# Gates between the heads' pairs, setup steps at other places, forgetting logits in float32r, and squares summed by TensorE

## The chip, the cores and the metric

The kernel runs on one core of one Trainium2 chip, as one launch. The metric is the device time in microseconds. Before the change it is 1714.79 us, the median of three runs (1713.35 to 1715.84).

## The reference

The input is one sequence of 256 tokens with 1024 features. Two blocks follow each other, each with two layers, in fp32.

```
first block, per layer:
  mod = c @ mod_w + mod_b                -> six vectors: shift, scale, gain, twice
  h = rmsnorm(x)*(1+scale) + shift ; p = h @ w_in
  sparse attention: 8 heads of 64 over the 64 keys of highest score; the score is a
    weighted sum of relu(q_i . k_i) over 8 indexer heads
  forgetting attention: 8 heads of 64, logits = q.k/8 + cum[q] - cum[k], causal,
    cum = running sum of log_sigmoid(f + bias)
  x += gain * (sigmoid(g_a)*y_a + sigmoid(g_b)*y_b) @ w_out
  x += gain * (silu(conv a) * conv b of rmsnorm(x) @ w_up) @ w_down
x = rmsnorm(x)
second block, per layer:
  h = rmsnorm(x) @ w_in_2, and from it five branches: gated linear recurrence (forward and
    backward), conformer convolution, short convolution, window attention, cross attention
    to a memory of 256 tokens
  x += rmsnorm((sum over branches of sigmoid(h @ w_gate) * (y @ w_branch)) @ w_out)
```

## The kernel before, in words

Activations lie with features on the partitions: `x` is 128 x 8 x 256. Every large product takes its operands as a high and a low part in float32r: `w_hi`, `w_lo` for weights and `h_hi`, `h_lo` (or `a_`, `y_`, `o_`, `m_`) for activations. `linear` (L1213 to L1219) issues three matmuls per 128 rows: high by high, low weight by high, high weight by low; one output tile of 128 columns of a 1024-row matrix is 24 matmuls of 128x256. `token_major` (L1251 to L1257) does the same with weights as the moving side. Small products are fp32 matmuls; the profile shows each of them as two records.

Weights come from HBM in chunks of 1 MB into a ring of five, all issued by SP in one order (L1171), each when the chunk five before it has been used. Two blocks of eight 128x128 tiles are in a chunk. ScalarE copies a block into `w_hi` (L1496), VectorE subtracts it into `w_lo` (L1819), six blocks ahead of their use; both do that in `split_to`, before the work of each step. Modulation weights are chunks of their own: a step `mod` multiplies a quarter (256 outputs) straight from the ring with 16 records (L1292), ScalarE copies the result to `modacc` (L1536), and `modred` sums it over partitions by matmuls with ones (L1302), 16 records for the eight columns of one vector; VectorE adds the bias.

One function, `plan()`, writes a single list of steps; each engine walks it and does its part of each step in that order. A step claims one of seven PSUM banks in turn, and waits until the bank's result of seven claims before has been taken (`wait_taken`).

- **Start.** `stats` squares x on ScalarE (L1524) and GpSimd adds five squares into `mean` (L1117); `root` sums that and the three other squares over partitions (L1275, L1278), and ScalarE (Ln L1530, Exp L1532) and VectorE (L1901 to L1907) make 1/sqrt. `norm` then makes `h_val` (VectorE L1926, the last of eight tiles by GpSimd), `h_hi` (ScalarE L1552) and `h_lo` (VectorE L1922), and the first four token-major products run as one group, for which the low halves of blocks 0 to 3 must stand. ACT_TABLE_LOAD stands in `root` (L1528).
- **Tables.** The step `setup` comes behind three pairs of token-major products. VectorE writes `rel_rep` (L1854), then angles; TensorE multiplies the buckets (L1265, fp32, 32 rows), VectorE adds into `line`, ScalarE takes the sines.
- **First block's attention.** After the pairs `qa` and the first value pair come `cum` (TensorE L1320 to L1322, for which VectorE writes `lf`, L1980) and `decay2` (VectorE, L1991: eight `lhs` tiles of 16 partitions); then the indexer (L1331), q and k tiles of the forgetting attention (`qkf`, ScalarE L1602 into `h_val`) with a `topk` on VectorE after each four. `att` issues the logits of four pairs of heads (L1344, for the forgetting attention followed by L1346, the 16-row bias product), VectorE masks and reads them out (L2048), ScalarE takes exp. 16 gate tiles (`gate1`, 24 matmuls each) are filled in: two between the two forgetting attentions, three in each `att_out`, one behind each of the last two `att_turn`. After each second gate one modulation quarter follows.
- **Second block.** The layer's input norm squares x as it is updated; VectorE (for the first layer) or GpSimd (for the second) adds the squares. The products `hf` of the recurrence follow the last `att_turn` (L1380, transposes of `o_tm`) and the gate `az`.

## Time and profile before

| what | value |
|---|---|
| median of three runs | 1714.79 us |
| profiled execution | 1720.28 us |
| its span, first to last instruction | 1718.5 us |
| TensorE busy | 1589.4 us, 92% |
| VectorE / ScalarE / GpSimd busy | 66% / 48% / 3% |
| mean granted clock of TensorE | 0.943 of 2.4 GHz |
| read from HBM | 284.75 MB, 167 GB/s |

Matmuls overlap in the pipeline, so the start-to-start distance of two rows tells the pace better than the duration of one. A granted clock of 1.00 is 2.4 GHz, 0.50 is 1.2 GHz; a value between is a mean over a stretch with both. Idle time in brackets at the end of a timeline row is that of the engine just before the row, with what ended it.

### The profile page before, as it was taken

How to read it: one execution, taken by the hardware profiler on the slowest of the kernel's cores; microseconds unless marked ns; L12 is line 12 of the kernel's file. 1: busy time of each engine (PE TensorE's matmuls, PEld its weight loads, DVE VectorE, ACT ScalarE, POOL GpSimd, SP SyncE). 2: the span in 40 equal slices, each digit the busy share in tenths (PEclk: the TensorE clock that was granted, in tenths of full speed). 3: DMA queues.
4: the chain of work that ended last, by engine and by line, in shares of the span. 5: the costliest groups of instructions: out<-in, count | busy, mean ns of one | idle time of the engine just before them, and what ended most of it. 6: DMA issues, size and time to landing. Idle time of an engine off the chain costs nothing. (4 is left out here: it accounts for less than half of the span.)

```text
span 1718.5 us, 31556 instructions
## 1 busy us (share of the span) xinstructions
PE 1589.4 (92%) x12784; PEld 1499.6 (87%) x12784; DVE 1139.0 (66%) x2133; ACT 822.8 (48%) x1496; POOL 59.4 (3%) x64
## 2 busy tenths in 40 slices
PE   4799999899988999998999989899999698999997
PEld 2687899899987878998999979899999598998997
DVE  2556446788634663467987686967777559677874
ACT  3353444555434434445555564464445553644453
POOL 1000000000010000000000110000000200000001
PEclk8797999999998978999999999999999899999999
DMA  9443355456463533553664544244345432443430
GB/s 394 167 161 149 145 195 184 149 219 215 174 269 144 199 142 128 198 196 129 240 221 180 189 165 154 99 172 148 123 159 185 147 123 75 172 155 140 154 142 25
DMA packets 42048, 288.89 MB, mean 168 GB/s; under 512 B 4624, under 2 KB 6672, under 8 KB 7472
## 3 DMA queue, kind: packets, MB, share of 16 engines
q1 hardware_dynamic: 38880, 280.83, 44.1%
q10 hardware_dynamic: 3024, 6.03, 1.0%
q8 instruction: 103, 1.69, 0.4%
q14 instruction: 41, 0.34, 0.1%
HBM read 284.75 MB, written 2.10 MB: 167 GB/s over the span
## 5 line engine op out<-in xcount | busy, mean ns | idle before, releaser
L1819 DVE TENSOR_TENSOR w_lo<-ring,w_hi 128x1024 fp32r<-128x1024 f32 x436 | 527.6, 1232 | 331.1 <-ACT w_hi L1496 330.2
L1213 PE MATMUL bank<-h_hi,w_hi 128*128 128x256 f32 x2256 | 643.3, 292 | 12.6 <-ACT h_hi L1552 8.5
L1214 PE MATMUL bank<-h_hi,w_lo 128*128 128x256 f32 x2256 | 633.8, 288 | 0.0
L1219 PE MATMUL bank<-h_lo,w_hi 128*128 128x256 f32 x2256 | 584.4, 288 | 0.0
L1496 ACT ACTIVATE w_hi<-ring 128x1024 fp32r<-128x1024 f32 x436 | 447.6, 1053 | 102.3 <-PE bank L1219 101.9
L1213 PEld LDWEIGHTS bank<-h_hi,w_hi 128*128 128x128 f32 x2256 | 445.0, 197 | 24.2 <-issue 20.9
L1214 PEld LDWEIGHTS bank<-h_hi,w_lo 128*128 128x128 f32 x2256 | 445.1, 197 | 0.5 <-issue 0.5
L1219 PEld LDWEIGHTS bank<-h_lo,w_hi 128*128 128x128 f32 x2256 | 415.5, 197 | 0.0
L1251 PE MATMUL bank<-w_hi,h_hi 128*128 128x256 f32 (+1 forms) x304 | 88.7, 297 | 16.3 <-DVE w_lo L1819 12.7
L1213 PE MATMUL bank<-a_hi,w_hi 128*128 128x256 f32 x352 | 100.4, 285 | 0.5 <-DVE w_lo L1819 0.5
L1214 PE MATMUL bank<-a_hi,w_lo 128*128 128x256 f32 x352 | 99.2, 282 | 0.0
L1219 PE MATMUL bank<-a_lo,w_hi 128*128 128x256 f32 x352 | 99.1, 282 | 0.0
L1252 PE MATMUL bank<-w_lo,h_hi 128*128 128x256 f32 (+1 forms) x304 | 87.3, 292 | 0.0
L1213 PE MATMUL bank<-y_hi,w_hi 128*128 128x256 f32 x304 | 83.8, 282 | 0.0
L1214 PE MATMUL bank<-y_hi,w_lo 128*128 128x256 f32 x304 | 82.9, 279 | 0.0
L1257 PE MATMUL bank<-w_hi,h_lo 128*128 128x256 f32 (+1 forms) x304 | 80.2, 291 | 0.0
L1219 PE MATMUL bank<-y_lo,w_hi 128*128 128x256 f32 x304 | 78.9, 281 | 0.0
L1251 PEld LDWEIGHTS bank<-w_hi,h_hi 128*128 128x128 f32 x304 | 61.8, 203 | 19.5 <-issue 19.3
L1663 ACT ACTIVATE conv_a<-bank,sm 128x256 f32<-128x256 f32 x44 | 24.8, 563 | 105.9 <-PE bank L1219 105.9
L1292 PE MATMUL bank<-ring,c_wide 128*32 128x256 f32 x768 | 56.7, 418 | 20.1 <-DMA ring<-weights 20.1
L1213 PEld LDWEIGHTS bank<-a_hi,w_hi 128*128 128x128 f32 x352 | 67.3, 191 | 4.1 <-issue 3.3
L1219 PEld LDWEIGHTS bank<-a_lo,w_hi 128*128 128x128 f32 x352 | 67.2, 191 | 0.0
(326 smaller groups left out, 2397.5 us busy)
## 6 DMA issues: line engine op xcount, KB each, us to landing
ring<-weights SPq DMA_DIRECT2D x266, 1024.0 KB, 4.9
pos_bias<-scratch ACTq DMA_DIRECT2D x4, 512.0 KB, 4.7
x<-x_t ACTq DMA_DIRECT2D x1, 1024.0 KB, 6.2
scratch<-line ACTq DMA_DIRECT2D x1, 1024.0 KB, 5.1
mem_x<-mem_t ACTq DMA_DIRECT2D x1, 1024.0 KB, 7.0
out_t<-x SPq DMA_DIRECT2D x2, 512.0 KB, 2.6
co<-const SPq DMA_DIRECT2D x1, 461.5 KB, 6.7
levels_f<-levels ACTq DMA_DIRECT2D x1, 448.0 KB, 13.3
```

Source lines behind the costliest of these rows:

```text
L1213: pe.matmul(to, WH[:, b % SPLIT, o, :], hi[:, k, :], start=(i == 0), stop=False)
L1214: pe.matmul(to, WL[:, b % SPLIT, o, :], hi[:, k, :], start=False, stop=False)
L1219: last = pe.matmul(to, WH[:, b % SPLIT, o, :], lo[:, k, :], start=False, stop=(i == n - 1))
L1251: pe.matmul(o, q, WH[:, s:s + m.n, k, :], start=(k == 0), stop=False)
L1252: pe.matmul(o, q, WL[:, s:s + m.n, k, :], start=False, stop=False)
L1257: last = pe.matmul(o, q, WH[:, s:s + m.n, k, :], start=False, stop=(k == KD - 1))
L1292: m = pe.matmul(to[q:q + 32, 0:256], cpad[:, k, :], w[:, k, :], start=(k < 4), stop=(k >= 4), tile_position=(0, q))
L1496: act.activation(WH[:, b % SPLIT], ring_half(b), ACT.Copy).then_inc(w_hi, 1)
L1663: act.activation(to[:, st.j % 3, :], bank[u.bank][:, 0:S], ACT.Identity, scale=ss(("conv_w", st.l, 2), c), bias=ss(("conv_b", st.l), c)).t ...
L1819: ve.tensor_tensor(WL[:, b % SPLIT], ring_half(b), WH[:, b % SPLIT].bitcast(F32), ALU.subtract).then_inc(w_lo_v, 1)
```

## The change

1. **Start.** The scale (g=1) is computed before the shift (g=0); `modred` sums two columns after each quarter. The root comes after the scale, and `vals` makes VectorE's seven `h_val` tiles right behind it; only `h_hi` and GpSimd's tile wait for the shift. Blocks 0 to 3 are asked for and split before the third quarter of the shift.
2. **Tables.** VectorE's part is a step of its own, one pair earlier.
3. **Running sum.** `cum` and `decay2` move behind the first indexer and the second value pair. They now carry 32 rows: high and low parts of cum, in float32r.
4. **Forgetting logits.** q and k are kept as high (ScalarE) and low (VectorE) float32r parts: three 64-row matmuls and one 32-row matmul per head instead of two fp32 ones. The bank of a q or k tile is released by VectorE.
5. **Gates.** One behind the first and third pair of heads in each forgetting attention; two instead of three in each `att_out` of the sparse attention. 16 in all as before.
6. **Squares.** Where the norm's input comes row by row from VectorE (both input norms of the second block), TensorE sums all eight squares. ACT_TABLE_LOAD stands before the first square in place of the root.
7. **Recurrence.** The two forward `hf` tiles come before the last `att_turn`.

```diff
+            if mid and mid[hp]:
+                mid[hp]()
...
+        in_row = bool(after) and isinstance(after[0], tuple)
+        state["all_by_pe"][i] = in_row
...
-    for g in (0, 1):
+    for g in (1, 0):
         for part in range(4):
             mod(0, g, part)
-        if g == 0:
+            shifted = p.full_bank()
+            p.add("modred", ps=shifted, l=0, g=g, part=part, after=state["parts"][-1:])
+        state.update(summed=None, parts=[])
+        if g == 1:
             root(x_stats, "mod")
-        reduce_mod()
+            p.add("vals", mode="mod", l=0, which=0, hn=0, src="x")
...
         p.together(firsts.pop("tm"))
+        if l == 0:
+            p.add("setup_tables")
         ev = ev + pair("tm", qi[2:4], what="qi", q=1)
...
-        bcum = p.full_bank()
-        p.add("cum", ps=bcum, l=l)
-        p.add("decay2", l=l, ps=bcum, turned=turned_a)
...
         idx(0)
         v_taken = v_taken + pair("tm", vf[2:4], what="vf", q=1)
+        bcum = p.full_bank()
+        p.add("cum", ps=bcum, l=l)
+        p.add("decay2", l=l, ps=bcum, turned=turned_a)
         idx(1)
...
-        f0 = att("fox", l, 0, 8, P, 0, qk, v_taken)
-        gate(), gate()
-        f1 = att("fox", l, 1, 8, 2 * P, 1, qk, v_taken)
+        f0 = att("fox", l, 0, 8, P, 0, qk, v_taken, [gate, None, gate, None])
+        f1 = att("fox", l, 1, 8, 2 * P, 1, qk, v_taken, [gate, None, gate, None])
...
-        att_out(s0, [gate, gate, gate])
+        att_out(s0, [gate, gate])
         ots.append(att_turn(f1, 4))
-        att_out(s1, [gate, gate, gate])
+        att_out(s1, [gate, gate])
...
+        hf = [fm("hf", t["hff"][j], dir=0, j=j, l=l).ps for j in range(2)]
         q1 = att_turn(w1, 0)
...
-        st.upto = min(st.first + SPLIT, len(p.blocks)) - 1 if begun else 1 if st.kind == "norm" else -1
+        first_ones = st.kind == "mod" and st.g == 0 and st.part >= 2 or st.kind == "norm"
+        st.upto = min(st.first + SPLIT, len(p.blocks)) - 1 if begun else 3 if first_ones else -1
...
-                pe.wait_ge(sq_sum, ADDED * (st.i + 1))
-                pe.matmul(sums[:, 0:S], ones, mean2[:], start=True, stop=False)
-                for k in range(ADDED + 1, KD):
+                if st.n is not None:
+                    pe.wait_ge(sq_sum, ADDED * (st.n + 1))
+                    pe.matmul(sums[:, 0:S], ones, mean2[:], start=True, stop=False)
+                for k in range(0 if st.n is None else ADDED + 1, KD):
                     pe.wait_ge(sq_done, KD * st.i + k + 1)
...
-                    m = pe.matmul(o, q(h), k(h), start=True, stop=(st.name != "fox"))
                     if st.name == "fox":
-                        m = pe.matmul(o, lhs16[:, h, st.t * P:st.t * P + P], rhs16[:, 0:st.W], start=False, stop=True)
+                        (qh, ql), (kh, kl) = q(h), k(h)
+                        pe.matmul(o, qh, kh, start=True, stop=False)
+                        pe.matmul(o, qh, kl, start=False, stop=False)
+                        pe.matmul(o, ql, kh, start=False, stop=False)
+                        m = pe.matmul(o, lhs32[:, h, st.t * P:st.t * P + P], rhs32[:, 0:st.W], start=False, stop=True)
...
             def stat(st):
+                if st.k == 0:
+                    act.preload_act_table_set("natural_log_exp_and_others")
...
+                    if st.early is not None:
+                        wait_taken(act, st.early)
...
+            def vals(st):
+                v, hi, lo, rs, gain = output_of(st)
+                own.wait()
+                for k in range(KV):
+                    ve.scalar_tensor_tensor(v[:, k, :], src_of(st.src)[:, k, :], gain(k)[0], rs[:], ALU.mult,
+                                            ALU.mult).then_inc(hval_v, 1)
...
+            def qkf(st):
+                if st.l == 0 and st.what == "q" and st.j == 0:
+                    ve.wait_ge(line_out, 16)
+                low, high, scale = (QL, QH, 0.125) if st.what == "q" else (KL, KH, 1.0)
+                ve.wait_ge(qk_hi, 8 * st.l + (4 if st.what == "k" else 0) + st.j + 1)
+                ve.scalar_tensor_tensor(low[:, st.j, :], bank[st.ps.bank][:, 0:S], scale, high[:, st.j, :].bitcast(F32),
+                                        ALU.mult, ALU.subtract).then_inc(taken[st.ps.bank], 1)
```

## Rows read from the trace of the kernel before

**Rows 1.** The page: busy shares, and TensorE's clock in 40 slices.
```profile
PE 1589.4 (92%) x12784; PEld 1499.6 (87%) x12784; DVE 1139.0 (66%) x2133; ACT 822.8 (48%) x1496; POOL 59.4 (3%) x64
...
PEclk8797999999998978999999999999999899999999
```

**Rows 2.** Waits of TensorE: releaser, us in total, times, longest.
```profile
PE bank L1251 <- DVE w_lo L1819: 12.7, 1, 12.7
PE sums L1275 <- POOL mean L1117: 12.5, 1, 12.5
PE bank L1380 <- DVE o_tm L1824: 12.3, 6, 3.3
```

**Rows 3.** Timeline of the start: start us, duration us, engine, line, operation [idle before].
```profile
26.81 1.07 PE L1292 MATMUL bank<-ring,c_wide 128*32 128x256 f32 x16 [1.75 <-DMA ring<-weights]
...
31.43 3.55 PE L1302 MATMUL bank<-co,modacc 128*128 128x1 f32 x16 [0.57 <-ACT modacc L1536]
31.51 1.06 ACT L1496 ACTIVATE w_hi<-ring 128x1024 fp32r<-128x1024 f32 x1 [0.22 <-DMA ring<-weights]
...
38.15 0.91 ACT L1552 ACTIVATE h_hi<-h_val,modv 128x256 fp32r<-128x256 f32 x2 [4.64 <-DVE h_val L1926]
...
47.69 0.55 PE L1251 MATMUL bank<-w_hi,h_hi 128*128 128x256 f32 x1 [12.71 <-DVE w_lo L1819]
```

**Rows 4.** Timeline of the tables, VectorE and TensorE.
```profile
71.44 0.62 DVE L1854 COPY rel_rep<-sm 32x128 f32<-32x128 f32 x4
...
72.11 7.19 PE L1265 MATMUL bank<-bucket_of,rel_rep 32*128 32x512 f32 x8 [4.45 <-DVE rel_rep L1854]
```

**Rows 5.** Timeline of TensorE: indexer, then forgetting attention of 128 and 256 columns.
```profile
107.02 1.26 PE L1331 MATMUL bank<-qi_t 64*128 64x128 f32 x16
...
141.34 0.46 PE L1344 MATMUL bank<-h_val 64*128 64x128 f32 x2 [0.67 <-ACT h_val L1602]
...
145.04 0.48 PE L1346 MATMUL bank<-rhs,lhs 16*128 16x128 f32 x2
...
159.31 0.70 PE L1344 MATMUL bank<-h_val 64*128 64x256 f32 x2
...
161.81 0.70 PE L1344 MATMUL bank<-h_val 64*128 64x256 f32 x2
```

**Rows 6.** Stretches: length, busy by engine (instructions), granted clock, DMA share, GB/s.
```profile
47.70:53.20 5.50, 5.50 (x26) 5.50 (x27) 2.00 (x2) 0.18 (x1) 0.00 (x0) 0.50 0.83 310
128.90:140.70 11.80, 11.77 (x100) 11.56 (x96) 10.64 (x35) 4.70 (x8) 0.00 (x0) 1.00 0.47 187
...
159.30:175.00 15.70, 15.70 (x37) 6.88 (x33) 4.68 (x14) 2.82 (x7) 0.00 (x0) 0.60 0.35 135
175.00:179.70 4.70, 4.70 (x24) 4.70 (x24) 1.27 (x6) 3.38 (x14) 0.00 (x0) 0.51 0.00 0
617.60:652.60 35.00, 34.97 (x129) 22.40 (x129) 17.80 (x64) 8.02 (x23) 0.00 (x0) 0.63 0.33 121
```

**Rows 7.** Timeline of the running sum and of VectorE after topk(0).
```profile
106.27 0.38 PE L1320 MATMUL bank<-co,lf 128*16 128x128 f32 x2 [2.98 <-DVE lf L1980]
...
138.00 3.49 DVE L1819 TENSOR_TENSOR w_lo<-ring,w_hi 128x1024 fp32r<-128x1024 f32 x3
...
143.25 0.11 DVE L2018 MEMSET score<- 64x64 f32 x1
153.49 0.28 DVE L2048 CUSTOM_DVE_ANT_0 logits<-bank,co 128x128 f32<-128x128 f32 x1
```

**Rows 8.** Timeline of the second layer's input norm, second block.
```profile
1363.02 1.15 ACT L1524 ACTIVATE h_val<-x 128x256 f32<-128x256 f32 x3 [0.25 <-DVE x L1824]
...
1366.98 1.19 PE L1275 MATMUL sums<-mean,co 128*128 128x256 f32 x2 [12.49 <-POOL mean L1117]
...
1370.77 0.47 ACT L1530 ACTIVATE guess<-sums,co 128x256 f32<-128x256 f32 x1 [5.30 <-PE sums L1278]
```

**Rows 9.** Timeline of TensorE at the last turn of the first layer's window attention.
```profile
1114.90 0.66 PE L1380 MATMUL bank<-co,o_tm 128*128 128x128 f32 x2 [2.86 <-DVE o_tm L1824]
```

More of the change, by code:

```diff
@@ L211, in some_mod, with att @@
             mod(l, g, part)
-    def att(name, l, t, H, W, slot, after, values):
+    def att(name, l, t, H, W, slot, after, values, mid=()):
         a = p.count("att")
@@ L270, in root @@
     def root(i, mode):
-        p.add("root", i=i, atts=p.counts.get("att", 0), mode=mode)
+        p.add("root", i=i, n=None if state["all_by_pe"][i] else state["added"][i], atts=p.counts.get("att", 0), mode=mode)
     def norm(kind, after, src, i=None, rooted=False, **more):
@@ L744, in constants @@
     for h in range(8):
-        lhs[8 + h, h] = 1.0
-        lhs[h, 8 + h] = 1.0
+        lhs[[16 + h, 24 + h], h] = 1.0
+        lhs[[h, 8 + h], 8 + h] = 1.0
     put("sel_lhs", lhs)
+    low = np.zeros((P, 1), np.float32)
+    low[8:16], low[24:32] = -1.0, -1.0
+    put("sel_lo", low)
     lev = np.zeros((P, 7, P), np.float32)
@@ L890, in program @@
         R = place("rot", [P, NT, 20, DH], 0)
-        lhs16 = place("lhs16", [16, 8, S], 0)
+        hb = place("h_val", [P, KD, S], 72960)
+        lhs32 = place("lhs32", [32, 8, S], 0, F32R)
         OH = place("o_hi", [P, 8, S], 0, F32R)
@@ L1093, in heads_q @@
             if st.name == "fox":
[L1094 removed]
+                return (lambda h: [m[half(h), h // 2, t * P:t * P + P] for m in (QH, QL)],
+                        lambda h: [m[half(h), h // 2, 0:W] for m in (KH, KL)],
                         lambda k, h: Vf[:, k, h * DH:h * DH + DH])
@@ L1103, in heads_q @@
                     lambda k, h: Va[:, k, :])
-        def by_vector(st):
-            return isinstance(st.after, tuple) and st.after[0] == "xn"
         def add_square(engine, st):
+            if st.n is None:
+                return
             engine.wait_ge(sq_done, st.i * KD + st.k + 1)
@@ L1273, in root @@
                     pe.wait_ge(o_norm, st.atts)
-                pe.wait_ge(sq_sum, ADDED * (st.i + 1))
-                pe.matmul(sums[:, 0:S], ones, mean2[:], start=True, stop=False)
-                for k in range(ADDED + 1, KD):
+                if st.n is not None:
+                    pe.wait_ge(sq_sum, ADDED * (st.n + 1))
+                    pe.matmul(sums[:, 0:S], ones, mean2[:], start=True, stop=False)
+                for k in range(0 if st.n is None else ADDED + 1, KD):
                     pe.wait_ge(sq_done, KD * st.i + k + 1)
-                    m = pe.matmul(sums[:, 0:S], ones, hb[:, k, :], start=False, stop=(k == KD - 1))
+                    m = pe.matmul(sums[:, 0:S], ones, hb[:, k, :], start=(st.n is None and k == 0), stop=(k == KD - 1))
                 m.then_inc(sums_ready, 1)
@@ L1300, in modred @@
                     wait_taken(pe, u)
-                for j in range(KD):
+                for j in red_cols(st):
                     m = pe.matmul(to[:, j:j + 1], modacc[:, j // 2, (j % 2) * P:(j % 2 + 1) * P], ones[:, 0:1],
@@ L1318, in cum @@
                 pe.wait_ge(decay_ready, st.l + 1)
-                pe.matmul(to[0:16, 0:P], lf16[:, 0, :], upto1[:, 0:P], start=True, stop=True)
-                pe.matmul(to[0:16, P:S], lf16[:, 0, :], upto1[:, P:2 * P], start=True, stop=False)
-                pe.matmul(to[0:16, P:S], lf16[:, 1, :], upto1[:, 0:P], start=False, stop=True).then_inc(ready, 1)
+                lf = [lf32[:, t].rearrange("p r h -> p (r h)") for t in range(NT)]
+                pe.matmul(to[0:32, 0:P], lf[0], upto1[:, 0:P], start=True, stop=True)
+                pe.matmul(to[0:32, P:S], lf[0], upto1[:, P:2 * P], start=True, stop=False)
+                pe.matmul(to[0:32, P:S], lf[1], upto1[:, 0:P], start=False, stop=True).then_inc(ready, 1)
             def idx(st):
@@ L1600, in qkf @@
                 wait_ready(act, st.ps)
-                to = qf if st.what == "q" else kf
+                to = QH if st.what == "q" else KH
                 act.activation(to[:, st.j, :], bank[st.ps.bank][:, 0:S], ACT.Copy,
-                               scale=0.125 if st.what == "q" else 1.0).then_inc(taken[st.ps.bank], 1)
+                               scale=0.125 if st.what == "q" else 1.0).then_inc(qk_hi, 1)
             def gate1(st):
@@ L1890, in modred @@
                 wait_ready(ve, st.ps)
-                tt(modv[:, st.l, st.g, :], bank[st.ps.bank][:, 0:KD], ss(("mod_b", st.l, st.g), 0, KD),
+                j = slice(red_cols(st).start, red_cols(st).stop)
+                tt(modv[:, st.l, st.g, j], bank[st.ps.bank][:, j], ss(("mod_b", st.l, st.g), 0, KD)[:, j],
                    ALU.add).then_inc(taken[st.ps.bank], 1)
@@ L2372, in m2end @@
                 m2_low(st.l, KD - 1)
-            do = dict(setup=setup, modred=modred, root=root, norm=norm, stat=stat, rope=rope, decay=decay,
-                      cum=cum, decay2=decay2,
+            do = dict(setup_tables=setup_tables, setup=setup, vals=vals, modred=modred, root=root, norm=norm,
+                      rope=rope, decay=decay,
+                      cum=cum, decay2=decay2, qkf=qkf,
                       idx=idx, topk=topk, lg=lg, ex=ex, tp=tp, no=no, ot=ot, y1=y1, wo1=wo1, dn=dn, up=up, upend=upend,
```

97 lines of the change are left out of this document (55 added, 42 removed).

## The prediction

> **What bounds the kernel now.** I read the page first: TensorE (PE) is busy 92% of the span and VectorE (DVE) 66% [rows 1], so time can leave in three ways only: TensorE's idle stretches, its stretches at the lower clock level, and work taken off it. The waits of TensorE, read next, are few and named: 12.7 us until the first weights' low halves stand, 12.5 us for GpSimd's sum of squares, 12.3 us in six waits for `o_tm` [rows 2]. The clock line has many 7s and 8s: the level falls to 1.2 GHz wherever TensorE idled or ran small matmuls. The windows give its price: dense work takes 5.5 us for 26 matmuls at level 0.50 (0.212 us each) and 11.8 us for 96 big ones and a modulation quarter at 1.00 (0.12 each) [rows 6]. The timeline was read last, at each place that the change touches. All sums below are made in the frame of the profiled execution, span 1718.5 us, run 1720.28; the runs' median is 1714.79, 5.5 below it, and I take the differences off the median.
>
> **The start.** Before, eight modulation quarters land ahead of the first weights: the matmuls wait for a chunk every 2.4 us, the weights' first chunk is there at 31.5, `h_hi` starts at 38.15, and only behind it does ScalarE make the high halves of blocks 2 to 5, and DVE their low halves; TensorE starts at 47.69 [rows 3]. After, two weight chunks land seventh and eighth and are split during the modulation, and DVE makes seven `h_val` before the shift is known (7 x 0.47). What is last is then the shift's last quarter, the tenth chunk: 31.5 + 2.4 = 33.9. Behind it stand one modulation step (1.07 to 1.9), ScalarE's copy (0.38), two of eight column sums (a quarter of 3.55, 0.9), DVE's addition (0.17), the semaphores between them (0.1 each) and `h_hi` (0.5): TensorE starts at 37.5 to 38.9. The tenth chunk also waits for the slot of the fifth, which is free only after the root's sums (the chain of three waits per quarter moves TensorE back); that may add 1.5. I take 38.5: **-9 us** (bounds -7 and -10.5). DVE isn't late: 3.3 us of `h_val` and 4.7 of low halves fit between 27 and 36.
>
> **The tables.** `rel_rep` stands at 71.44 behind six low halves, and TensorE, idle since 67.7, then runs 7.2 us of 32-row matmuls and 3 us of dense ones at the lower level [rows 4]. After, the tables come behind four low halves (two fewer, 2.4 us): the idle time falls from 4.45 to 1.7, -2.8. DVE's tables (4.6 us) now precede the last two low halves, the sines and the four `line` additions, but TensorE next needs DVE only at the transposes 16 us on. With the clock kept, the matmuls take about half of 7.2 and the next steps 1 to 2 us less; it may still fall, since they are small. I take half of that 5.2: **-5.5** (bounds -2.8 and -8).
>
> **The running sum** (`cum`) moves behind the second value pair. DVE's `lf` stands behind two low halves, which stand behind two high halves: 4.2 us from the pair's end, of which 1.25 were covered by transposes and 2.98 idle [rows 7]. Now nothing covers it: 4.2 idle, +1.3 per layer. `decay2` gets two ops more (0.45 each) and delays the scores.
>
> **Forgetting attention.** Before, a head is two fp32 matmuls of 64 and 16 rows. Nine of them start within 3.7 us for 128 columns (0.415 each) and four within 2.5 for 256 (0.625 each) [rows 5]: 0.21 us more for 128 more columns, so 0.205 is fixed, paid where shapes alternate. After, a head is three 64-row float32r matmuls and one of 32 rows. The trace has none of these shapes; dense float32r starts every 0.12. Lower bound 4 x 0.12 = 0.48; upper bound, the fixed part in each, 4 x 0.325 = 1.3. I take it twice per head, as there are still two changes of shape: 0.48 + 0.41 = 0.89. Both halves are 7.1 us each for eight heads, against 8.5 and 15.7 measured, much of it at the lower level (mean 0.60 in the second) [rows 6].
> Where it starts: the low halves of q and k are 16 DVE ops of 0.47 reading PSUM, and the bank is free only after them. Four queue behind topk(0), which ends at 138.0, with the low halves of weights: 138.5 + 4 x 1.65 = 145.1, against 141.34 before [rows 5, 7]. TensorE, done at 141.8, idles 3.3 us instead of 0.7. The second topk runs from 146.3 to 156.5 (10.2 us as before); the first bank is wanted again at 158.9, after DVE has read it. From 145.1: two halves 14.2, four gates of 24 matmuls 11.6, two modulation steps 2.1: 173.0, against 175.0 with two gates and one step; 6.9 us of later work is done, and the gate behind no longer runs slowly (4.7 us for 24 matmuls [rows 6], 1.8 above full speed). At full clock that is -10.7 per layer. The idle time will lower the level and pairs between gates may again: I charge 3.3, and 0.5 for the two later places that have lost a gate. **-7 per layer, -14 in all**; the two layers look alike (33.7 and 35.0 us [rows 6]). Bounds per layer: -11, and +1 if the mean level stays near 0.62 throughout.
> The Trainium skill, "TensorE: Matmul & The Clock Gate" (Step-by-step: what each phase is for), says that a weight load is pulled ahead of running matmuls where the row groups don't conflict. By it the heads in the upper 64 rows would load beside the bias product in the lowest rows (rival e).
>
> **Squares summed by TensorE.** In the second block the last square is done at 1364.2, TensorE waits for GpSimd's sums until 1366.98, and four matmuls follow at the lower level until 1370.7; Ln starts at 1370.77 [rows 8]. After, eight matmuls of 0.43 (0.86 at the lower level) follow the squares from 1359: eight slow ones end at 1366.4. The table load in the root (1.28, then Ln at once) moves ahead of the squares: another 1.2 off. Ln at 1365.3: **-5.4** (bounds -3 and -7). The sibling near 1005 swaps 1.9 us of DVE adds for a table load ahead of the squares and four more matmuls: +0.5 (bounds -2 and +2). Elsewhere the load hides partly behind sums: -0.4 twice and -0.2 at the end, **-1**.
> The Trainium skill, "ScalarE: Activation LUTs" (What ACT_TABLE_LOAD costs), adds a drain of 1.38 us to a switch; by it this term would be 1.4 larger. The trace shows Ln 0.01 us behind the load, so I don't.
>
> **The recurrence's first products.** Two linear tiles (5.8 us) now stand before the last turn, where TensorE waited 2.86 us for `o_tm` in the first layer [rows 9] and 3.29, the longest of the six such waits [rows 2], in the second. `o_tm` is done 3.2 us after the last value matmul, so both waits go: **-6.1** (bounds -5 and -6.5). The queue is the same: sixteen chunks before and after.
>
> **Sum.** -9 - 5.5 - 14 - 5.4 - 1 + 0.5 - 6.1 = -40.5: 1674.3 us.
>
> **Rivals.**
> (a) The fixed part is paid by each matmul: 1.3 per head, 6.6 us more per layer, or DVE's queue (66% busy, now 7.5 us more per layer) eats the same: 1688. For: no such shapes in the trace. Against: the indexer's eight 64-row fp32 matmuls, all of one shape, take 1.26 us together [rows 5], 0.157 each, so it isn't paid where the shape stays. 0.22.
> (b) The clock stays up in the tables and in both attentions, as gates lie between the pairs: the 6.6 and 2.5 charged come back: 1665. Against: the idle 3.3 us. 0.15.
> (c) Slower: spread gates and waits keep the level at 1.2 GHz through the whole first-block attention (about 100 us per layer at full clock). Each slow us gives up 0.44 (0.12 against 0.212), so from 46 us more at the low level per layer the gain is gone; for the whole region it costs 78 us per layer, over 1800. Against: before, the level rose again within 5.5 us of dense matmuls each time. 0.03.
> (d) The change only moves waits: TensorE's work is nearly kept, what is won at the start is lost to a later landing. Against: the DMA engines are busy 47% of a dense stretch and 83% of the one right behind the start [rows 6], so they have room to catch up: about 1714, 0.02.
> (e) Heads in the upper 64 rows pay no fixed part beside bias weights in the lowest rows: half of 16 heads x 0.41 is 3.3 per layer, 1668. Against: in the old trace upper and lower pairs alike start every 0.415 [rows 5]. 0.03. This is where the rule above would bring it.
> My forecast, 1664 to 1684: 0.55.
> The range runs to the cases (a) and (b): 1661 to 1690. A difference within 0.2% (3.4 us) can't be told from none. Faster 0.94, same 0.03, slower 0.03.
>
> **What would show it.** The first dense matmul at 37.5 to 39; an idle time of 1.5 to 2 before the bucket matmuls; heads of 0.8 to 1.0 us in the first attention, its start 3 us after the last k tile, behind DVE's low part; no wait of GpSimd in TensorE's list; Ln of the second block 5 us sooner after the z root; no `o_tm` wait of 3 us. Wrong it would be if heads take over 1.2 us, if the first attention starts later than 5 us after the last k tile, if the granted clock there stays near 0.6, or if the first dense matmul is later than 41.

## The result and the profile after

The changed kernel takes 1668.72 us, the median of 4 runs (1666.87 to 1673.13), beside 1715.32 (1713.35 to 1716.14, 4 runs) of the kernel before on the same chip: a ratio of 0.9734 (0.9713 to 0.9755). Forecast were 1674.3 us in 1661 to 1690. Run again with the experiments the same kernel took 1677.38 (1667.37 to 1686.87, 6 runs), 0.9785 (0.9754 to 0.9816); how its times follow the granted clock is told below, and why the clock differs between executions stays open. The profiled executions took 1720.28 and 1666.87.

The page of the changed kernel, beside [rows 1]:

```profile
PE 1561.2 (94%) x12800; PEld 1483.2 (89%) x12800; DVE 1142.2 (69%) x2162; ACT 821.1 (49%) x1495; POOL 57.0 (3%) x60
...
PEclk9899999999998999999999999999999899999999
```

TensorE is busy 28 us less with no less to do, and most 7s and 8s of its clock line are gone: the mean granted clock is 0.969 instead of 0.943.

TensorE's waits after (releaser, us in total, times, longest), beside [rows 2]. GpSimd's 12.5 us and the wait of 12.7 for `w_lo` are gone, and `o_tm` has 4 waits instead of 6. The sums now wait for ScalarE's squares, 9.7 us. The wait for `lf` has grown from 6.0 to 8.5, and the one for `kf_lo` is new:

```profile
PE sums L1302 <- ACT h_val L1556: 9.7, 4, 5.1
PE bank L1345 <- DVE lf L2019: 8.5, 2, 4.2
...
PE bank L1410 <- DVE o_tm L1857: 6.4, 4, 1.7
PE bank L1371 <- DVE kf_lo L2048: 4.8, 2, 2.4
```

The wait for `lf` in the kernel before:

```profile
PE bank L1320 <- DVE lf L1980: 6.0, 2, 3.0
```

The start, beside [rows 3]. The dense work (the large three-part products) starts at 42.14 instead of 47.69. TensorE waits for ScalarE's copy of the third quarter at 36.58, since that copy (36.07) stands behind four `w_hi`; the column sums of the last quarter start at 40.02:

```profile
32.28 3.88 ACT L1526 ACTIVATE w_hi<-ring 128x1024 fp32r<-128x1024 f32 x4
36.07 0.37 ACT L1567 ACTIVATE modacc<-bank 128x256 f32<-128x256 f32 x1
...
33.03 1.70 PE L1316 MATMUL bank<-ring,c_wide 128*32 128x256 f32 x16
36.58 0.98 PE L1326 MATMUL bank<-co,modacc 128*128 128x1 f32 x4 [1.85 <-ACT modacc L1567]
37.50 1.93 PE L1316 MATMUL bank<-ring,c_wide 128*32 128x256 f32 x16
40.02 0.98 PE L1326 MATMUL bank<-co,modacc 128*128 128x1 f32 x4 [0.60 <-ACT modacc L1567]
42.14 0.55 PE L1274 MATMUL bank<-w_hi,h_hi 128*128 128x256 f32 x1 [1.13 <-ACT h_hi L1585]
```

One head of the forgetting attention at full clock (one pair of heads follows another at the same distance), beside [rows 5]: from 144.10 to 144.83, 0.73 us for four matmuls. Before, a head was 0.83 (two at 0.415).

```profile
144.10 0.32 PE L1371 MATMUL bank<-kf_hi,qf_hi 64*128 64x128 f32 x1
144.26 0.27 PE L1372 MATMUL bank<-kf_lo,qf_hi 64*128 64x128 f32 x1
144.37 0.27 PE L1373 MATMUL bank<-kf_hi,qf_lo 64*128 64x128 f32 x1
144.57 0.32 PE L1374 MATMUL bank<-rhs,lhs 32*128 32x128 f32 x1
144.83 0.32 PE L1371 MATMUL bank<-kf_hi,qf_hi 64*128 64x128 f32 x1
```

Both forgetting attentions with their four gates, one stretch per layer (columns as in [rows 6]; there the mean clock stood at 0.60 in the second attention, f1, of the first layer, and at 0.63 over both in the second layer). f0 is the attention of the first 128 tokens, f1 that of all 256:

```profile
138.20:168.20 30.00, 30.00 (x209) 25.09 (x209) 19.59 (x66) 9.39 (x27) 0.00 (x0) 0.94 0.37 138
600.50:629.10 28.60, 28.56 (x209) 23.77 (x209) 19.65 (x66) 9.35 (x27) 0.00 (x0) 1.00 0.39 145
```

The second layer's input norm of the second block, beside [rows 8]: no wait for GpSimd. `x` comes from VectorE every 0.67 us, ScalarE squares it, and TensorE's sixteen records end 1.9 us after ScalarE's last square; the table load of 1.28 us is over before the first square. From the previous Ln to the first dense matmul it takes 1310.85 to 1325.32.

```profile
1311.78 1.28 ACT L1541 ACT_TABLE_LOAD   x1
...
1315.90 5.79 PE L1302 MATMUL sums<-h_val,co 128*128 128x256 f32 x16 [5.09 <-ACT h_val L1556]
...
1321.73 0.47 ACT L1561 ACTIVATE guess<-sums,co 128x256 f32<-128x256 f32 x1 [1.95 <-PE sums L1302]
...
1325.32 0.36 PE L1236 MATMUL bank<-h_hi,w_hi 128*128 128x256 f32 x1 [3.63 <-ACT h_hi L1587]
```

**Ledger.** At marks ahead of which both kernels have done equal work, the lead of the changed one (start times of the two profiled executions, their difference, and what the stretch added). The execution of before took 1720.28 us, more than any of the 38 in the table below, and that of the changed kernel 1666.87, the fastest of its ten; so the ledger shows 53 us where the medians of all executions differ by 43:

| mark | before | after | lead | added |
|---|---|---|---|---|
| first dense matmul | 47.69 | 42.14 | 5.5 | 5.5 |
| end of the first value pair | 102.03 | 92.33 | 9.7 | 4.2 |
| third turn of heads, 14 gates done | 242.2 | 225.3 | 16.9 | 7.2 |
| first dense matmul of the second layer | 536.63 | 515.28 | 21.3 | 4.4 |
| third turn of heads, second layer | 720.3 | 686.0 | 34.3 | 13.0 |
| turn of the cross attention, second block | 1087.3 | 1049.7 | 37.6 | 3.3 |
| first dense matmul, its second layer | 1374.37 | 1325.32 | 49.0 | 11.4 |
| end of TensorE's work | 1707.2 | 1654.1 | 53.1 | 4.1 |

### The profile page after: what moved, and what is told of

Its sections match the earlier page's. It is cut to its first block and busy times, and to the rows that moved or that the text cites. A ratio compares the mean times of both kernels' runs of the same rounds, so it can differ in the third digit from the quotient of the medians.

```text
span 1665.1 us, 31606 instructions
## 1 busy us (share of the span) xinstructions
PE 1561.2 (94%) x12800; PEld 1483.2 (89%) x12800; DVE 1142.2 (69%) x2162; ACT 821.1 (49%) x1495; POOL 57.0 (3%) x60
## 5 line engine op out<-in xcount | busy, mean ns | idle before, releaser
L1236 PE MATMUL bank<-h_hi,w_hi 128*128 128x256 f32 x2256 | 636.9, 290 | 11.7 <-ACT h_hi L1585 7.4
L1237 PE MATMUL bank<-h_hi,w_lo 128*128 128x256 f32 x2256 | 626.7, 285 | 0.0
L1236 PEld LDWEIGHTS bank<-h_hi,w_hi 128*128 128x128 f32 x2256 | 438.1, 194 | 23.7 <-issue 19.9
L1237 PEld LDWEIGHTS bank<-h_hi,w_lo 128*128 128x128 f32 x2256 | 438.2, 194 | 0.5 <-issue 0.5
L1242 PEld LDWEIGHTS bank<-h_lo,w_hi 128*128 128x128 f32 x2256 | 409.2, 194 | 0.3 <-DVE h_lo L1857 0.2
L1237 PEld LDWEIGHTS bank<-a_hi,w_lo 128*128 128x128 f32 x352 | 66.2, 188 | 0.0
```

The costliest lines, as they stand in the source:

```text
L1236: pe.matmul(to, WH[:, b % SPLIT, o, :], hi[:, k, :], start=(i == 0), stop=False)
L1237: pe.matmul(to, WL[:, b % SPLIT, o, :], hi[:, k, :], start=False, stop=False)
L1242: last = pe.matmul(to, WH[:, b % SPLIT, o, :], lo[:, k, :], start=False, stop=(i == n - 1))
```

## The experiments

All edits are to the changed kernel unless the text says otherwise. Groups of one to four kernels ran on one chip each, with the kernel before beside them. The changed kernel was run beside its own result and again in the group of the column sums (two blocks split) and the two running-sum kernels, but not in the other three; the kernel before had medians from 1711.98 to 1716.72 in all of them. Because the times turned out to depend on the granted clock of each execution, each run is read with it: the time at the lower level is 2 x (1 - mean clock) x span. Over the ten executions of the changed kernel that time ran from 103 to 158 us and the execution time from 1666.87 to 1686.87. A straight line with one slope for all 13 kernels and one intercept for each (95 executions) has a slope of 0.33 us per us at the lower level, and what is left scatters by 1.7 us. Two executions are left out: one of 2175.31 us at a mean clock of 0.642 (column sums later, two blocks split), and one of 1671.78 us whose clock of 0.925 fits no line (and topk(0) sooner). The table has both parts; "rest" is the intercept, an extrapolation to the time of that kernel with no us at the lower level. A difference of two rests is good to about 2.3 us (95%). The level is less sure: that of the changed kernel was 108 us the first time (4 executions) and 131 the second (6), so a difference of means against it is good to some 15 us, or 5 us of time.

| kernel | executions | median us | at lower level, mean us | rest us |
|---|---|---|---|---|
| before | 38 | 1714.3 | 184 | 1652.9 |
| changed | 10 | 1671.1 | 122 | 1632.6 |
| fp32 heads | 4 | 1688.0 | 148 | 1636.9 |
| gates in old places | 4 | 1680.3 | 144 | 1632.2 |
| both | 4 | 1691.2 | 159 | 1638.8 |
| old start | 4 | 1678.0 | 130 | 1635.3 |
| small parts undone | 4 | 1693.2 | 145 | 1644.8 |
| running sum behind idx(1) | 4 | 1674.8 | 121 | 1634.9 |
| and topk(0) sooner | 3 | 1683.1 | 141 | 1633.8 |
| column sums later, two blocks split | 3 | 1683.4 | 149 | 1631.2 |
| lf early | 6 | 1663.0 | 109 | 1626.3 |
| lf early, sums later, topk(0) sooner | 6 | 1659.9 | 116 | 1621.1 |
| lf early, sums later, topk behind k and f0 | 5 | 1651.9 | 105 | 1617.4 |

### Forgetting attention: heads and gates

```diff
-pe.matmul(o, qh, kh, ...); pe.matmul(o, qh, kl, ...); pe.matmul(o, ql, kh, ...)
-m = pe.matmul(o, lhs32[:, h, ...], rhs32[:, 0:st.W], ...)
+m = pe.matmul(o, q(h), k(h), start=True, stop=False)
+m = pe.matmul(o, lhs16[:, h, ...], rhs16[:, 0:st.W], start=False, stop=True)
```

> The changed kernel with the forgetting logits in fp32 again (two fp32 matmuls per head, no low halves of q and k), the gates still between the pairs. Theory A (most of the gain is the price of a head): heads cost 1.06 us instead of 0.73 with 128 columns and 1.25 instead of 0.82 with 256, +6.1 us per layer; the wait for the low half of k (2.4 us) shrinks to about 0.7, -1.7; in all +4.4 per layer, 1677 to 1679, and the heads run at a high granted clock. Rival B (the gain is the clock level, and fp32 heads lose it even with gates between them): f1 costs another 5 to 6 us per layer as it did before, +20 in all, 1687 to 1690.

```diff
-f0 = att("fox", l, 0, 8, P, 0, qk, v_taken, [gate, None, gate, None])
-f1 = att("fox", l, 1, 8, 2 * P, 1, qk, v_taken, [gate, None, gate, None])
+f0 = att("fox", l, 0, 8, P, 0, qk, v_taken)
+gate(), gate()
+f1 = att("fox", l, 1, 8, 2 * P, 1, qk, v_taken)
```

> The changed kernel with the gates where they stood: none between the pairs of heads, two between f0 and f1, three (not two) in each sparse att_out. Theory A (the short float32r heads keep TensorE busy enough by themselves): within 1.5 us of the changed kernel, 1667 to 1671. Rival B (the gates between the pairs hold the clock level): f0 and f1 run partly at the lower level, +3 per layer, 1674 to 1677.

> The changed kernel with both undone: fp32 forgetting logits and the gates in their old places. If price and clock add: the difference to the changed kernel is the sum of the two runs with one undone. My blind value for both together was 14 us (1683); the trace of the changed kernel says 22 to 26 (its stretch from the end of the last k tile is 10 to 13 us per layer shorter at equal work): 1691 to 1695. If the two interact (gates help only fp32 heads) it is more than the sum of both.

The first of these runs also takes back what belongs to the low halves on VectorE: `qf_lo`, `kf_lo`, two of the four `lf` operations and the parts of the running sum.

Measured: 1688.03 (ratio 0.9833, 0.98 to 0.9867), 1680.31 (0.9797, 0.977 to 0.9823) and 1691.22 us (0.9865, 0.9839 to 0.9891). The stretch of both forgetting attentions in the second layer, of fp32 heads with gates between, float32r heads without, and fp32 heads without:

```profile
608.00:652.00 44.00, 44.00 (x214) 33.59 (x214) 18.75 (x67) 12.51 (x39) 0.00 (x0) 0.70 0.31 119
```

```profile
608.00:640.00 32.00, 30.66 (x141) 25.16 (x142) 19.93 (x71) 8.54 (x27) 0.00 (x0) 0.64 0.36 132
```

```profile
608.00:640.00 32.00, 32.00 (x128) 21.06 (x128) 17.62 (x67) 7.87 (x25) 0.00 (x0) 0.67 0.31 117
```

The clock column reads 0.70, 0.64, 0.67, against 1.00 in the changed kernel. (The stretches hold a little more or less of the gates, so their lengths aren't compared.) But 1.00 is not what float32r heads with gates between them always show. Ten profiled executions here have both (the changed kernel twice, and the eight kernels below that keep them), and in each the attentions of two layers can be read: from the first head to the last the mean clock lies between 0.75 and 1.00, or 0 to 18 us at the lower level, 9.6 on average. With one or both undone it lies between 0.64 and 0.73, 19 to 24 us. The two halves differ. f1 takes 15.83 us at full clock in 16 of these 20 stretches. f0 runs partly at the lower level in 18 of them, with a mean clock of 0.70 to 0.88, and at 1.00 only in the second layer of the two executions of the changed kernel. So the two together raise the level, mostly in f1, and neither fp32 heads between gates nor float32r heads in a row do as well.

By the table the price of the heads is 4.3 us in all (1636.9 against 1632.6) and their clock 8.7 (26 us at 0.33). The gates cost no work (1632.2) and their clock is 7.3 (22 us), each clock term with the 5 us of doubt said above. The times of both runs lie nearer to rival B than to theory A: fp32 heads within its 1687 to 1690, the gates above its 1674 to 1677. Both undone are 18.4 us of rest and clock together (6.2 and 12.2), nearly the sum of the two (19.9), so no interaction can be told from the scatter; by medians they are 20.1 against 17.0 and 9.2.

What a row of heads does to the level is seen without idle time in f1 without gates. TensorE had not waited since 138.24 and worked at full clock from 152.85 on. Three heads take 0.86 us each, the level falls at 159.60 in the fourth, and from 160.41 on a head takes 1.44; L1372 is the first of the four rows of a head:

```profile
156.69 0.38 PE L1372 MATMUL bank<-kf_hi,qf_hi 64*128 64x256 f32 x1
...
157.55 0.38 PE L1372 MATMUL bank<-kf_hi,qf_hi 64*128 64x256 f32 x1
...
160.41 0.58 PE L1372 MATMUL bank<-kf_hi,qf_hi 64*128 64x256 f32 x1
...
161.85 0.58 PE L1372 MATMUL bank<-kf_hi,qf_hi 64*128 64x256 f32 x1
```

In f0 a wait stands ahead, so it can't be read that way: 2.41 us without gates, 2.40 in the changed kernel, and in the first layer of both kernels the level falls in the second head, 0.9 to 1.0 us behind the wait. There the gates make the other half of the difference: in the changed kernel's first profile the level is back at 142.57, within the first gate. Without gates all eight heads pass first, to 147.37, the first two in 0.70 and 1.07 us, each later one in 1.23; the level is back at 152.85, in the second of the two gates behind them:

```profile
138.69 0.32 PE L1375 MATMUL bank<-rhs,lhs 32*128 32x128 f32 x1
138.94 0.33 PE L1372 MATMUL bank<-kf_hi,qf_hi 64*128 64x128 f32 x1
...
141.23 0.47 PE L1372 MATMUL bank<-kf_hi,qf_hi 64*128 64x128 f32 x1
...
142.46 0.47 PE L1372 MATMUL bank<-kf_hi,qf_hi 64*128 64x128 f32 x1
```

### The same kernel again, and the old start

> The changed kernel itself once more, unedited, as the yardstick beside the others on this chip, and as a second profiled execution. Theory A (the granted clock in the forgetting attention is held by the change): time 0.971 to 0.976 of before; TensorE at the lower level for about 105 us in all, as in its first profile, and for at most 3 us per layer between the last k tile and the first value matmul. Rival B (the level there varies from execution to execution, as the kernel with the old start showed, where it fell four times in the first layer): the same ratio, but 125 to 150 us at the lower level, and another stretch of f0 or f1 low.

Measured: 1677.38 us, 0.9785 (0.9754 to 0.9816). The two stretches of its profiled execution:

```profile
132.40:165.50 33.10, 33.05 (x209) 28.09 (x209) 19.68 (x66) 9.48 (x27) 0.00 (x0) 0.85 0.34 126
601.00:629.70 28.70, 28.56 (x209) 23.78 (x209) 19.75 (x66) 9.45 (x27) 0.00 (x0) 1.00 0.40 146
```

The same 209 matmuls took 33.1 us at 0.85 and 30.0 at 0.94 in the first profile; the second layer held 1.00 twice. So in the changed kernel theory A holds for the second layer and rival B for the first; in the eight kernels derived from it f0 of the second layer ran partly low too. The level at the same place differs although program and matmuls are the same. The six times spread over 19.5 us and their clock over 0.953 to 0.967.

```diff
-for g in (1, 0):
+for g in (0, 1):
     for part in range(4):
         mod(0, g, part)
-        shifted = p.full_bank()
-        p.add("modred", ps=shifted, l=0, g=g, part=part, after=state["parts"][-1:])
...
+    if g == 0:
+        root(x_stats, "mod")
+    reduce_mod()
...
-st.upto = ... if begun else 3 if first_ones else -1
+st.upto = ... if begun else 1 if st.kind == "norm" else -1
```

> The changed kernel with the old start: vector 0 before vector 1, one modred of eight columns per vector, weights' first chunk only for the norm, h_val after the shift. Theory A (what the start gives stays to the end): the first dense matmul moves from 42.1 back to 47.7, +5.5, 1674. Rival B (my blind value of 9 was right and something at the changed kernel's start hides it): +8 to +9, 1677. Rival C (the DMA engines or the tables eat it): +2 or less.

Measured: 1678.04 us, 0.9788 (0.9761 to 0.9815). The first dense matmul is at 45.9, 3.7 us later than in the changed kernel and not 5.5: in this execution the column sums of eight columns took 1.92 us at full clock, where [rows 3] has 3.55. Beside the changed kernel's ten executions the median is 6.9 us more; by the table 2.7 are rest and 2.7 clock. Its profile had the level fall in the forgetting attentions of both layers (0.75 and 0.85 from first head to last) though gates and heads were as in the changed kernel. The first layer:

```profile
141.80:180.00 38.20, 38.18 (x216) 32.83 (x217) 20.92 (x72) 9.77 (x28) 0.00 (x0) 0.74 0.34 131
```

A rest of 2.7, good to 2.1 us, goes with the 3.7 of the trace and with the 2 or less of rival C; it can't tell between them, and it leaves no room for +9, rival B. The traces put the start at 3.7 to 5.5 us, by the level at which the old one ran.

### The small parts

Undone together: the tables' place, the running sum's, the table load's, TensorE's sum of squares and the recurrence's first products. The running sum again stands ahead of idx(0). GpSimd adds the squares for both second-block norms here, where VectorE did so for the first of them before; TensorE waits 7.6 us there against 6.3 before.

```diff
 ev = ev + pair("tm", qi[2:4], what="qi", q=1)
+p.add("setup_tables")
...
+p.add("cum", ps=bcum, l=l)
+p.add("decay2", l=l, ps=bcum, turned=turned_a)
...
-in_row = bool(after) and isinstance(after[0], tuple)
+in_row = False
...
-hf = [fm("hf", t["hff"][j], dir=0, j=j, l=l).ps for j in range(2)]
+hf = [fm("hf", u[2 * i + j], dir=i, j=j, l=l).ps for i in range(2) for j in range(2)]
```

> The changed kernel with its small parts undone together: the tables behind the third pair, the running sum at its old place, the table load in the root, GpSimd adding the squares of the first two second-block norms as everywhere else, the recurrence's first products behind the last turn. New start, float32r heads and gates between the pairs stay. Each place is read by itself. By my sum: rel_rep idle 4.45 instead of 1.44 and bucket matmuls as slow (+3 to +5.5); running sum idle 3.0 instead of 4.25 (-1.3 per layer); second layer's first norm +5.4; last turn's waits 2.9 and 3.3 us (+6.1); table load +1: 14 to 16 more in all, 1686 at the same level. Rival: the squares' new place is worth less, as TensorE's eight matmuls wait for ScalarE's squares (9.7 us in four waits), so only +2 to +3 there.

Measured: 1693.16 us, 0.9882 (0.9854 to 0.991): 22 above the changed kernel, 12.2 of it rest. Its waits:

```profile
PE sums L1298 <- POOL mean L1136: 20.1, 2, 12.5
...
PE bank L1409 <- DVE o_tm L1855: 12.9, 6, 3.3
...
PE bank L1344 <- DVE lf L2017: 6.3, 2, 3.2
...
PE bank L1287 <- DVE rel_rep L1885: 4.3, 1, 4.3
```

Each wait is back in its old place and size: `rel_rep` 4.3 instead of 1.4, `o_tm` 12.9 instead of 6.4 (-6.5, forecast -6.1), `lf` 6.3 instead of 8.5. The one long wait for the squares is back too, 12.5 us. The rival fails: from the sums of `z` (the norm ahead) to the Ln of the norm behind it takes 16.3 us here and 10.9 in the changed kernel, 5.4 as forecast. The whole is 7 us above the 1686 forecast, which held the level fixed; 23 us more at the lower level, at 0.33, are that.

### The running sum, the start and topk

The ledger leaves 4.25 us per layer ahead of the running sum. I moved it, and then topk(0) on VectorE as well:

```diff
+idx(1)
 p.add("cum", ps=bcum, l=l)
 p.add("decay2", l=l, ps=bcum, turned=turned_a)
-idx(1)
```

> The changed kernel with the running sum and decay2 behind idx(1) instead of ahead of it. Theory A: the idle time of 4.25 us per layer ahead of the sum is covered by the sixteen matmuls of idx(1), which then also run at full speed (2.1 instead of 3.95 and 3.0): 4.2 minus 0 to 1 of idle, -3.5 to -4.2 per layer and another 1 to 2 by the clock: -8 to -12 in all. Rival B (DVE is the bound there): decay2 (4.5 us) now delays topk(0) and with it the low halves of k: the idle time turns up ahead of f0 (2.4 becomes 5 or more), less than 4 us gained.

```diff
 qk = [fm("qkf", qf[j], what="q", j=j, l=l).ps for j in range(2)]
+p.add("topk", t=0, l=l, W=P)
 qk += [fm("qkf", qf[j], what="q", j=j, l=l).ps for j in range(2, 4)]
-p.add("topk", t=0, l=l, W=P)
```

> As the kernel with the running sum behind idx(1), and topk(0) on VectorE's queue two q tiles sooner (behind q tile 1 instead of q tile 3). Theory A: the four low halves of k no longer queue behind topk(0); f0 starts without the wait of 2.40 us: another -2.4 per layer, about -5, and the clock is held in f0. Rival B: the low halves of q tiles 2 and 3 and of their weights queue behind topk(0) (7.3 us) instead, and TensorE waits for w_lo in the k tiles: nothing gained or lost beyond 1 us.

Measured: 1674.77 us (0.977, 0.9749 to 0.9791) and 1677.8 (0.9789, 0.9755 to 0.9823): nothing gained. Topk(0) sooner did shorten the wait ahead of f0, from 2.40 to 1.13 us. But on the running sum both theories of the first kernel failed: its wait grew to 6.3 us, and VectorE's queue shows why. `lf` (L2019) now stands behind the eight score operations of idx(1), here in the first of the two kernels:

```profile
99.56 0.35 DVE L2058 TENSOR_SCALAR score<-relu,wis 128x256 f32<-128x256 f32 x1
99.94 3.81 DVE L2061 SCALAR_TENSOR_TENSOR score<-relu,wis,score 128x256 f32<-128x256 f32 x7
103.67 0.43 DVE L2019 SCALAR_TENSOR_TENSOR lf<-fx,fln 128x16 f32<-128x16 f32 x4
```

Moving the step moved its operations on every queue. What `lf` needs had been there since 78.0 (ScalarE's Ln). So VectorE's four `lf` operations alone were moved, out of `cum` into a step behind the second rope (`grp=1`):

```diff
+p.add("forget", l=l)
-def cum(st):
+def forget(st):
     ve.wait_ge(f_log, st.l + 1)
```

> The changed kernel with VectorE's four lf operations as a step of their own behind the second rope (their inputs stand at 78 us in the first layer, the operations start at 105), the running sum's matmuls where the change put them. Theory A (lf is late only by its place in VectorE's queue): no idle time ahead of the running sum (4.25 us per layer gone) and idx(1) at full speed (2.1 us): -8.5 of idle, and 20 to 30 us less at the lower level, which at 0.34 us each is another -2 to -6 over the whole; 9 to 13 us less than the changed kernel at the same level elsewhere. Rival B: what is won turns up as idle time ahead of f0 (kf_lo behind topk(0)), which grows from 2.4 to 4 and more: net -5 or less.

Measured: 1662.97 us, 0.9703 (0.9678 to 0.9728); rest 6.3 less, level 13 us less. VectorE and TensorE in that kernel:

```profile
90.13 0.42 DVE L2020 SCALAR_TENSOR_TENSOR lf<-fx,fln 128x16 f32<-128x16 f32 x4
```

```profile
101.34 0.41 PE L1346 MATMUL bank<-co,lf 128*32 128x128 f32 x2
101.58 0.38 PE L1347 MATMUL bank<-co,lf 128*32 128x128 f32 x2
101.80 0.38 PE L1348 MATMUL bank<-co,lf 128*32 128x128 f32 x2
102.11 2.10 PE L1357 MATMUL bank<-qi_t 64*128 64x256 f32 x16
```

No idle time, and idx(1) in 2.10 us instead of 3.95. The wait ahead of f0 grew from 2.40 to 3.09 us, so of 8.5 us some 1.4 came back: theory A with a touch of B.

At the start I took the wait on ScalarE out of TensorE's chain, `modred` of a quarter behind `mod` of the next, first with two blocks split:

```diff
+if part < 4:
+    mod(0, g, part)
+if late:
+    p.add("modred", ps=shifted, l=0, g=late[0], part=late[1], after=late[2])
```

> The changed kernel with each quarter's column sums issued one modulation quarter later (as many matmuls, other order), and two blocks of weights instead of four split ahead of the norm. Theory A (the start is bound by the ring of three waits per quarter: matmuls, ScalarE's copy, column sums): TensorE no longer waits 0.5 to 1.85 us per quarter, eight quarters of 2.95 plus 3.9 of sums from 10.6: first dense matmul at 38 to 39 instead of 42.1, -3 to -4 us. Rival B (the quarters' chunks bind): first dense matmul at 41 to 42, less than 1 us gained. Rival C: two blocks fewer are split, and TensorE waits for w_lo later in the first value pair, nothing gained.

Measured: 1683.4 us, the median of three executions, 0.9803 (0.9775 to 0.983): rival C, and worse than thought. The level carries the loss, 149 us against 122; the rest is 1631.2 against 1632.6. The column sums end at 33.8, yet the first dense matmul is at 42.70, behind this wait; the first step takes tiles of all four blocks in turn:

```profile
PE bank L1279 <- DVE w_lo L1857: 8.9, 1, 8.9
```

With four blocks split, `lf` early and topk(0) two tiles sooner:

> lf early as in the kernel before this one, topk(0) two q tiles sooner on VectorE, and at the start the column sums one quarter later (with four blocks of weights split ahead of the norm, all of which the first matmuls want). Theory A: first dense matmul at 38 to 39 instead of 41 to 42 (-3), no idle time ahead of the running sum (-8.5), ahead of f0 1 us or less instead of 2.4 (-3): 14 us less idle time than the changed kernel; with the level kept, 1650 to 1662. Rival B (the start): ScalarE's copy of quarter 2 stands behind the four w_hi until 36, first dense matmul at 40.5 or later. Rival C: the level falls more often elsewhere and the time is not below 1665.

Measured: 1659.91 us, 0.9685 (0.9658 to 0.9712). The first dense matmul is at 39.71. The wait ahead of f0 is still 3.09, with topk(0) sooner or not: VectorE works without a pause from 98 us up to there, so the order of its work inside that stretch gained nothing. The last kernel takes topk out of it:

```diff
-p.add("topk", t=0, l=l, W=P)
...
 qk += [fm("qkf", kf[j], what="k", j=j, l=l).ps for j in range(4)]
-p.add("topk", t=1, l=l, W=2 * P)
+p.add("topk", t=0, l=l, W=P)
...
 f0 = att("fox", ...)
+p.add("topk", t=1, l=l, W=2 * P)
 f1 = att("fox", ...)
```

> lf early and the column sums one quarter later, as in the kernel of 1659.9; topk(0) behind the last k tile instead of two q tiles sooner, and topk(1) behind f0's last pair. In that kernel's trace VectorE works without a pause from 98 us to the last low half of k at 125, so TensorE's 3.09 us ahead of f0 are VectorE's throughput and not the place of one queue entry. Theory A: with the 7.2 us of topk(0) out of that stretch the low halves of k keep up with the k tiles: f0 starts 0.7 us or less behind them, -2.4 per layer, and the level holds there: 1653 to 1656. Rival B: the 17 us of topk turn up behind: TensorE waits for a bank that VectorE hasn't read or for w_lo within f0 and f1, 3 us or more per layer: no gain, 1660 or slower.

Measured: 1651.88 us (1649.08 to 1659.93, 5 runs), 0.9634 (0.961 to 0.9658). The wait ahead of f0 is 1.13 us, just one copy and one low half; no wait for a bank or `w_lo` shows up in f0 or f1:

```profile
121.94 0.38 ACT L1641 ACTIVATE kf_hi<-bank 128x256 fp32r<-128x256 f32 x1 [1.54 <-PE bank L1248]
...
122.36 0.42 DVE L2054 SCALAR_TENSOR_TENSOR kf_lo<-bank,kf_hi 128x256 fp32r<-128x256 f32 x1 [0.70 <-ACT kf_hi L1641]
...
123.04 0.29 PE L1377 MATMUL bank<-kf_hi,qf_hi 64*128 64x128 f32 x1 [1.13 <-DVE kf_lo L2054]
```

This version beats both kernels: its interval lies below that of either run of the changed kernel.

## Why the prediction came out right

The median lies 6 us below the forecast and inside the range, but the sum hides misses that offset each other: the start gave 3.5 us less than its term and the tables 1.3 less, the forgetting attention 6 more, and some 11 of the ledger are in no term. Of the signs it named, a first dense matmul later than 41 was one of being wrong, and it came (42.14). The heads, 0.73 and 0.85 us, lie at and just below the 0.8 to 1.0 it named; the waits and the Ln of the second block came as said. That the total came so near is in part luck.

**The start** was mis-sized: 5.5 us against 9 (bounds 7 and 10.5), first dense matmul 42.14 and not 37.5 to 39. The failed step is "behind it stand one modulation step, ScalarE's copy, two of eight column sums": I had counted the last quarter's chain from its chunk, at 33.9. But every quarter is such a chain. The four of the scale ran at the lower level: 1.94 of matmuls, 0.5 of waiting, 1.0 of sums, 3.4 per quarter where a chunk lands every 2.4. The shift's second took only 2.2, at full clock; its third took 4.5, as the copy behind four `w_hi` cost 1.3 (1.85 instead of 0.59). With ScalarE's waits taken off the chain the dense work starts at 39.71 and 39.34, and TensorE waits there for the chunks (1.4 and 0.9 us for the last two): 2.4 to 2.8 of the 3.5 us missing.

**The tables**: 4.2 against 5.5, inside the bounds; idle 1.44 against 1.7 forecast, but the clock stayed low, 6.39 us of matmuls instead of 7.19. I had given half to the clock; it gave 1.2.

**The running sum**: idle 4.25 as forecast (4.2). Not forecast: the idle time lowered the level, and idx(1) took 3.95 and 3.00 us instead of 2.10.

**Forgetting attention**: 20.2 by the ledger (7.2 and 13.0) against 14; the term was mis-sized, the mechanism right. The idle time ahead was 2.40, not 3.3; a head at full clock 0.73 us with 128 columns and 0.85 with 256, not 0.89 for both; and above all the charge of 3.3 per layer for the clock was due only in the first layer, where 3.5 us at the lower level in one profile and 10 in the other (0.94 and 0.85) are 1.5 and 4.4 us at 0.44 each. The second layer stood at 1.00 twice. That was a fortunate layer: with the same heads and gates the eight kernels derived from it were at 0.76 to 0.89 there. The premise that the level falls wherever TensorE runs small matmuls doesn't hold either: f1 kept it in 16 of 20 stretches. Rival (b) was nearly what the profiled execution shows, and the median of all ten, 1671.1, lies between it and my forecast. Rival (a) failed: 1.3 us per head never showed, not even at the lower level (1.23 with 128 columns). Rivals (c) and (d) did not come. Of rival (e) I see nothing: heads in the upper and the lower rows take 0.73 alike. The rule of the Trainium skill, "TensorE: Matmul & The Clock Gate" (Step-by-step: what each phase is for), on weight loads pulled ahead, from which (e) was argued, shows as no gain in any row here.

**Squares**: from the sums of `z` to the first dense matmul 14.5 us instead of 19.9, 5.4 as forecast. Its sibling in the first layer cost 0.5, as forecast: from the sums of the norm ahead to the first product with `mk_t` TensorE takes 37.1 us instead of 36.5. Table loads: the waits for `h_hi` ahead of `up` are 3.72 instead of 4.24, 0.5 each.

**The recurrence**: the waits of 2.86 and 3.29 us are gone, 6.1 forecast; the six waits' 12.3 us are four of 6.4, 5.9 less, and 12.9 when undone.

Together these are some 42. The ledger's other 11 us come mostly from stretches that the change hardly touches, where the execution of before ran at the lower level more often (mean clock 0.96 against 0.98 from the first layer's third turn to the second layer, 0.97 against 0.98 from the second layer's third turn to the cross attention, 0.95 against 0.98 from there to the second block's second layer); part of that is the choice of executions said at the ledger. About half of the whole gain is clock: over all executions 20.8 us (62 us at the lower level less, at 0.33), the other half, 20.3, is work and waits.

## What to carry to other kernels

Before crediting a change of a few microseconds, write down the granted clock of every execution beside its time: here 20 us between executions of one program lay on a straight line over it, to within 1.7 us. Profile a place more than once before calling its level shown: 1.00 in two executions of one kernel was 0.76 to 0.89 in its eight variants. Move the operations of one engine, not the whole step, when one of them is late: its inputs' time in the trace tells how early it can stand. Where an engine has no pause in the stretch that ends in a wait, reordering inside the stretch gained nothing here; taking work out of it did.

## What the runs showed of the hardware

- TensorE's level fell in a row of short matmuls though TensorE never idled: in f1 without gates it had been busy since 138.24, at full clock since 152.85, and fell at 159.60, from 0.86 to 1.44 us a head; in the second layer the same in the fourth head, from 630.57 on. With a dense tile of 24 matmuls behind the first and third pair it stayed up throughout f1 in 16 of 20 stretches, but throughout f0, which has a wait of 1.1 to 3.1 us ahead, in only 2 of 20.
- Whether it falls differs between executions of one program by up to 55 us of low level (103 to 158), about 20 us of time. The Trainium skill, "TensorE: Matmul & The Clock Gate" (What's actually happening), says that the number of slow matmuls at a kernel's start varies from run to run, and puts the penalty of that ramp below 1% of a typical span. Here the level falls at many places behind the start too: the spread alone is 1.2%, and the slow stretches are 6 to 9% of the span.
- A us at the lower level costs 0.33 us over 95 executions. In dense work it gives up 0.43 (a matmul every 0.212 us instead of 0.12), and half the clock would be 0.5. That idle time, which doesn't stretch, makes the difference is likely but not shown.
- float32r matmuls of 64 rows and 128 columns start 0.16 and 0.11 us apart within a head (144.10 to 144.26 to 144.37), 0.20 and 0.26 where the rows change from 64 to 32 and back (144.37 to 144.57 to 144.83); the fp32 pairs of 64 and 16 rows took 0.415 each.
